# Shorter lists searched from below, and bias-table transfers moved, in a two-block transformer kernel

## The reference, cut to what matters

```python
score = jnp.einsum('bqhk,bqh->bqk', jax.nn.relu(s), wib * idx_scale)
visible = key_chunk[None, :] <= qcb[:, None]
score = jnp.where(visible[None], score, NEG_INF)
_, sel = lax.top_k(score, k_top)                 # k_top = 256
valid = key_chunk[sel] <= qcb[None, :, None]
kg = gather(k, sel)
...
logits = jnp.where(valid[:, :, None, :], logits, NEG_INF)
```

```python
bias = rpb[:, (dr + NA_KH_MAX - 1)[None, :, None], (dc + kw - 1)[:, None, :]]
s = s + bias.astype(jnp.float32)[None]
```

## Time and profile before

| what | value |
|---|---|
| median of 3 runs | 3490.18 us (3487.72 to 3490.66) |
| the profiled execution's own time | 3484.2 us |
| its span | 3482.4 us |
| PE busy in the span | 3266.4 us (94%) |
| DVE busy | 1759.2 us (51%) |
| ACT busy | 1218.6 us (35%) |
| POOL busy | 1180.2 us (34%) |
| mean granted PE clock | 0.972 of full speed |

### The profile page before, as it was taken

One profiled execution on the slowest core, in us unless ns is written; L12 is line 12 of the kernel. 1 busy time (PEld: TensorE's weight loads), 2 busy tenths in 40 slices (PEclk: granted clock), 3 DMA queues, 4 the chain that ended last, 5 costly groups with the idle time before them and its releaser, 6 DMA issues. The chain is left out here.

```text
span 3482.4 us, 43824 instructions
## 1 busy us (share of the span) xinstructions
PE 3266.4 (94%) x17544; PEld 2854.7 (82%) x17544; DVE 1759.2 (51%) x2950; ACT 1218.6 (35%) x1847; POOL 1180.2 (34%) x844
## 2 busy tenths in 40 slices
PE   7899989998998999999998999989899899999997
PEld 6789989988887899999875788777787688888885
DVE  5579999553356799985435044433334321000014
ACT  5552211452265421225414154444423422222222
POOL 4316432115332373311343342311452433333232
PEclk9999999999999999999998999999999899999998
DMA  5111233104310112220141411111332111111111
GB/s 157 27 30 43 60 90 96 53 1 157 108 61 25 37 46 77 86 79 16 65 143 33 169 41 46 37 55 34 104 131 84 43 48 49 49 49 45 47 49 55
DMA packets 292159, 228.52 MB, mean 66 GB/s; under 512 B 37351, under 2 KB 266390, under 8 KB 291574
## 3 DMA queue, kind: packets, MB, share of 16 engines
q1 hardware_dynamic: 264278, 122.38, 13.0%
q0 software_dynamic: 21920, 82.13, 6.3%
q10 hardware_dynamic: 5760, 21.22, 1.5%
HBM read 175.31 MB, written 52.16 MB: 65 GB/s over the span
## 5 line engine op out<-in xcount | busy, mean ns | idle before, releaser
L670 PE MATMUL big<-H,wsp 128*128 128x348 f32 (+3 forms) x9600 | 1905.9, 358 | 70.7 <-POOL H L1786 25.1
L670 PEld LDWEIGHTS big<-H,wsp 128*128 128x128 f32 (+1 forms) x9600 | 1666.0, 191 | 277.1 <-issue 41.4
L1786 POOL TENSOR_TENSOR wsp<-raw,wsp 128x1024 fp32r<-128x1024 f32 (+2 forms) x246 | 542.8, 2207 | 1524.1 <-ACT wsp L1234 1513.4
L670 PE MATMUL big<-SP,wsp 128*128 128x512 f32 x1920 | 452.1, 396 | 0.0
L670 PEld LDWEIGHTS big<-SP,wsp 128*128 128x128 f32 x1920 | 360.3, 188 | 89.8 <-issue 0.7
L1234 ACT ACTIVATE wsp<-raw 128x1024 fp32r<-128x1024 f32 (+2 forms) x246 | 238.1, 968 | 516.3 <-PE big L670 369.2
L2473 DVE MAX8 top<-SC 128x8 f32<-128x272 f32 (+6 forms) x448 | 369.4, 825 | 0.0
L2479 DVE MATCH_REPLACE8 SC<-top,SC 128x272 f32<-128x272 f32 (+6 forms) x448 | 366.0, 817 | 0.0
L2633 DVE TENSOR_TENSOR X<-X,big 128x1024 f32<-128x1024 f32 (+1 forms) x26 | 29.6, 1139 | 478.1 <-PE big L670 478.1
L819 PE MATMUL small<-V,PT_a 128*128 128x64 f32 x1152 | 146.5, 272 | 0.1
L1282 ACT ACTIVATE rows_a<-rows_a,head_min 128x1040 f32<-128x1040 f32 (+8 forms) x130 | 101.6, 782 | 123.9 <-DVE head_min L2224 123.8
(11 more groups left out here) (316 smaller groups left out, 3590.4 us busy)
## 6 DMA issues: line engine op xcount, KB each, us to landing
raw<-in_w_in SPq DMA_DIRECT2D x108, 512.0 KB, 3.8
raw<-in_w_ff SPq DMA_DIRECT2D x64, 512.0 KB, 4.0
raw<-in_w_out SPq DMA_DIRECT2D x24, 512.0 KB, 5.3
gate_b_scratch<-tm POOLq DMA_DIRECT2D x16, 522.0 KB, 3.9
gate_a_scratch<-tm ACTq DMA_DIRECT2D x16, 522.0 KB, 2.8
tm<-gate_a_scratch POOLq DMA_DIRECT2D x16, 522.0 KB, 3.9
tm<-gate_b_scratch POOLq DMA_DIRECT2D x16, 522.0 KB, 4.7
tm<-xT_scratch POOLq DMA_DIRECT2D x16, 522.0 KB, 5.0
```

The costliest lines, as they stand in the source:

```text
L670: mm = pe.matmul(dst(o, width), w[wp][:, k, 0:cols], rhs(xp, k)[:, t0:t0 + width], start=(k == 0 and i == 0), stop=(k == rows - 1 and i == 2))
L1786: pool.tensor_tensor(dst, src, hi.bitcast(F32), ALU.subtract).then_inc(*S.inc(name, *key))
```

## The change

For blocks whose list is shorter than 512 (j = 1 and 2), the search runs on a copy. The copy is the negated scores in reversed order, in a free area that now has the name `low_scores`; it is searched for the keys to be left out, of which there are visible(j) - 256: 16 and 144, that is 2 and 18 rounds of 8. The mask is then read from the copy, reversed again, with the opposite comparison. Blocks 3 to 7 keep their 32 rounds. Reversing makes equal scores fall as before.

All three stages of the bias tables now stand behind one load, (ya, 1) of layer 0, whole: 3 pad transfers, a wait, 24 skewed ones, a wait, 24 strips. The load after them in SP's program is (ya, 2).

```diff
-        sb("z_rest", [P, (2 * KC * SEQ - KC * TP - 2 * TP - 9 * HD - SCORE_COLS)])
+        low_scores = sb("z_rest", [P, (2 * KC * SEQ - KC * TP - 2 * TP - 9 * HD - SCORE_COLS)])
...
-            band_steps = {nload[("mb", 0, 0)]: (lambda: rpb_pad())}
-            for i in range(6):
-                band_steps[nload[("mb", 0, 1)] + i] = lambda i=i: skewed_bands(tables[4 * i:4 * i + 4])
-                band_steps[nload[("mb", 0, 5)] + i] = lambda i=i: strip_bands(tables[4 * i:4 * i + 4])
+
+            band_steps = {nload[("ya", 0, 1)]: lambda: (rpb_pad(), skewed_bands(tables), strip_bands(tables))}
...
+                scores = {j: SC[:, SCORE_AT[j]:SCORE_AT[j] + visible(j)] for j in range(1, NQ)}
+                lowest = {j: visible(j) < 2 * TOPK for j in range(1, NQ)}
+                low_at = {j: sum(visible(i) for i in range(1, j) if lowest[i]) for j in range(1, NQ)}
+                searched = {j: low_scores[:, low_at[j]:low_at[j] + visible(j)] if lowest[j] else scores[j] for j in range(1, NQ)}
+                count = {j: (visible(j) - TOPK if lowest[j] else TOPK) // 8 for j in range(1, NQ)}
+                turned_keys = lambda ap, j: ap[:, visible(j) - 1::-1]
...
-                rounds = [(r, j) for r in range(TOPK // 8) for j in range(1, NQ)]
+                for j in range(1, NQ):
+                    if lowest[j]:
+                        wait(("mask_step", l, "hidden", j))
+                        dve.tensor_scalar(searched[j], turned_keys(scores[j], j), -1.0, None, ALU.mult)\
+                            .then_inc(*S.inc("mask_step", l, "turned", j))
+                rounds = [(r, j) for r in range(TOPK // 8) for j in range(1, NQ) if r < count[j]]
...
-                        dve.match_replace(sc, top8[:, j, :], sc, TAKEN).then_inc(*S.inc("taken", l, r, j))
+                        dve.match_replace(searched[j], top8[:, j, :], searched[j], TAKEN).then_inc(*S.inc("taken", l, r, j))
                 for j in range(1, NQ):
-                    sc = SC[:, SCORE_AT[j]:SCORE_AT[j] + visible(j)]
-                    wait(("taken", l, TOPK // 8 - 1, j))
-                    dve.tensor_scalar(sc, sc, TAKEN / 2, NEG, ALU.is_gt, ALU.mult).then_inc(*S.inc("mask_step", l, "made", j))
+                    wait(("taken", l, count[j] - 1, j))
+                    found = turned_keys(searched[j], j) if lowest[j] else searched[j]
+                    dve.tensor_scalar(scores[j], found, TAKEN / 2, NEG, ALU.is_lt if lowest[j] else ALU.is_gt, ALU.mult)\
+                        .then_inc(*S.inc("mask_step", l, "made", j))
```

More of the change, by code:

```diff
@@ L2471, in _ @@
                         r, j = rounds[x]
-                        wait(("taken", l, r - 1, j) if r else ("mask_step", l, "hidden", j))
-                        dve.max(top8[:, j, :], SC[:, SCORE_AT[j]:SCORE_AT[j] + visible(j)])\
-                            .then_inc(*S.inc("eight", l, r, j))
+                        wait(("taken", l, r - 1, j) if r else ("mask_step", l, "turned" if lowest[j] else "hidden", j))
+                        dve.max(top8[:, j, :], searched[j]).then_inc(*S.inc("eight", l, r, j))
                     if x >= 1:
                         r, j = rounds[x - 1]
-                        sc = SC[:, SCORE_AT[j]:SCORE_AT[j] + visible(j)]
                         wait(("eight", l, r, j))
-                        dve.match_replace(sc, top8[:, j, :], sc, TAKEN).then_inc(*S.inc("taken", l, r, j))
+                        dve.match_replace(searched[j], top8[:, j, :], searched[j], TAKEN).then_inc(*S.inc("taken", l, r, j))
                 for j in range(1, NQ):
-                    sc = SC[:, SCORE_AT[j]:SCORE_AT[j] + visible(j)]
-                    wait(("taken", l, TOPK // 8 - 1, j))
-                    dve.tensor_scalar(sc, sc, TAKEN / 2, NEG, ALU.is_gt, ALU.mult).then_inc(*S.inc("mask_step", l, "made", j))
+                    wait(("taken", l, count[j] - 1, j))
+                    found = turned_keys(searched[j], j) if lowest[j] else searched[j]
+                    dve.tensor_scalar(scores[j], found, TAKEN / 2, NEG, ALU.is_lt if lowest[j] else ALU.is_gt, ALU.mult)\
+                        .then_inc(*S.inc("mask_step", l, "made", j))
                 for j in range(1, NQ):
```

## The result

Over four runs of each the changed kernel takes 3470.77 us in the median (3463.19 to 3478.82), the kernel before 3490.42 (3487.72 to 3491.24). The ratio is 0.994, with a 95% interval of 0.9928 to 0.9952: 0.6% faster, where 3470.9 us and 0.55% were forecast. The changed kernel run again in a later batch gives 3465.75 against 3487.06, ratio 0.9941 (0.9927 to 0.9955).

The account below looks back on a forecast made before the run. PE, busy 94% of the span, was taken as the bound; 12.73 us (tables, layer 0) plus 6.51 (search, layer 1) made 19.24 off, forecasting 3470.9 us, own range 3467 to 3475, wider range 3466 to 3478.

Parts of the forecast that it names:

- The two costs and their coupling: Table transfers cost layer 0 12.73 us and hide its search; late search costs layer 1 6.51; both 19.2.
- the search's lateness in layer 1: Layer 1, unit 0's to unit 3's logits: PE waits for DVE's search, then runs on a slow clock; 6.51 us.
- Why the tables cost PE time: Layer 0's mb jobs: SP issues 24 skewed tables between weight loads, so PE waits for split weights; 12.73 us.
- The sum of the search: DVE, each layer: 37.1 us of search pairs dropped, 1.5 us of copies and reversed masks added; 35.6 us net.
- The chain on SP: Layer 0's attention: pads, skewed tables and strips take 97 us, ending at 702, before (ya, 2) is needed; no cost.
- the bound of 138: Layer 0's attention: table transfers on SP with the dearest issue each time, 138 us, ending at 743; margin 40 us.
- The slower rival: Layer 0: table transfers outlast the attention, (ya, 2) comes late; beyond 178 us PE pays; 205 us gives 3497.2; chance 0.03.
- The gate loads: POOL's four loads in layer 0's attention, 27.3 us slack; rival: delayed in series, giving back 10.7 us, 3481.6; chance 0.05.
- The rival that something comes back inside the attention: Layer 0's attention: traffic beside PE, ACT and DVE handovers gives back a third of the 12.7 us; 3475; chance 0.08.
- The level: Whole kernel: median run time forecast at 3470.9 us, 0.55% less, with its own range 3467 to 3475.

Follow-up runs that it names:

- Search alone: Changed kernel with the bias-table transfers put back among the mb jobs as in the kernel before; 3482.12 against 3487.06 us, ratio 0.9985.
- tables alone: Kernel before with only the table transfers moved behind load (ya, 1) of layer 0, search as before; 3480.92 against 3487.06 us, ratio 0.9983.
- The longer chains: Changed kernel with the skewed-table transfers made twice, 3467.7 us, and three times, 3531.22 us, against 3489.31 for the kernel before.

## Why the prediction was right

**The two costs and their coupling.** Held in all parts. Off the mb jobs 12.73 us were predicted and measured; off the search's lateness in layer 1 6.51 and 6.50. Search alone: 6.5 predicted, 5.2 measured; tables alone: 6.2 and 5.9; both: 19.2 and, from the ratio of 0.994, 20.9 (the medians differ by 19.65). Each made alone, the parts add up to 11.1 us, and together they bring some 20; the remainder, 6.5 predicted and 9 measured, with some 3 us of uncertainty on each part and 4 on the two together, is what the tables' 12.7 us had been hiding of layer 0's search. The timelines show it without the noise: the tables alone lose 5.05 us to it in layer 0, where I had taken layer 1's 6.5; the two stretches differ in that execution (20.54 against 1549.55 - 1527.69 = 21.86), with the same wait of about 3.3 us in each, and the 1.3 us come behind it, where PE's passes are slow for longer in layer 1.

**Why the tables cost PE time.** The prediction had the weights late because SP issues the tables between them; SP's rows in the kernel before bear that out, and show that it is the issuing and not the landing:

```profile
434.72 3.73 SPq L616 DMA_DIRECT2D raw<-in_w_in  x1
438.49 9.56 SPq L592 DMA_DIRECT2D band_scratch<-rpb_scratch  x4
448.11 2.81 SPq L616 DMA_DIRECT2D raw<-in_w_branch_b  x1
```

Four loads, two pairs of an mb and a yb job, take SP from 408.19 to 460.60, 26.2 us a pair, while PE, unhindered, needs 17.2 us for one (yb 0 at 403.05, yb 1 at 420.23). The load issued from 448.11 is split by ACT at 453.91, 3.0 us behind its issue. A load's own issue takes 2.8 to 3.9 us there and 0.37 in the changed kernel; what holds it is not shown.

**The sum of the search.** 35.6 us net were predicted. The masks' last step ends the search; before, then after:

```profile
619.82 0.56 DVE L2486 MEMSET SC<- 64x64 f32 x7
```

```profile
590.62 0.41 DVE L2498 MEMSET SC<- 64x64 f32 x5
```

Counted from yb 0 that is 216.77 us and 181.66, so 35.1 less. There are 180 MAX8 a layer, as said. The pairs were right (block 2's 14 pairs, less its copy, make the idle time 14.2 us longer, from 14.60 to 28.78; 14.3 less a copy was predicted). The copies were mis-sized: 0.5 us each, measured 2.06 for the two from start to start (274.49 to 276.55). Reading in reverse is not the reason: the second copy, reversed as well, takes 0.36 us for 400 columns. The masks read in reverse cost nothing more either: all seven take 3.06 us (587.56 to 590.62) where they took 3.19 (616.63 to 619.82), and the 0.25 us put on each of two was not needed.

**The chain on SP.** 97 us predicted, 98.9 measured (the bound of 138 adds up to 137.3, which changes nothing); from the next load's issue to ACT's split 88 us predicted (702 to 790.4), 85 measured. The longer chains show the margin's end: 170.6 us cost nothing, 246.9 us (608.56 to 855.41) made PE wait 62.5. Counted back one for one, the price begins at some 184 us of chain, where I had put 178. The slower rival is thus a real mechanism, a little farther away than it was put: the load landed in some 3 us where 7 were allowed, and PE's need comes 3.6 us behind ACT's. A long landing of the 32 B runs did not show: landing stays within 5.6 us behind the last issue (615.15 + 73.14 to 693.88).

**The gate loads.** Landed within 7.9 us beside the tables (8.2 in the version with the tables alone), 7.0 without; DVE reads at 676.6 what was issued by 642.3, so over 26 us of slack were left. The rival that something comes back inside the attention has nothing for it: with and without the transfers the stretch agrees to 0.2 us wherever it takes its short time.

**The level.** That 3470.9 meets 3470.8 so closely is luck: the changed kernel spreads over 15.6 us in its first four runs. What I took as its own uncertainty, 3467 to 3475, was too narrow for a single run; the median of the first four lies in it, and that of the five of the later batch, 3465.75, does not. There the kernel before was 3.4 us faster as well, and the ratio is the same.

## What to carry to other kernels

When a kernel runs the same program twice and only one pass has an extra, lay the two timelines side by side from one shared instruction to the next: the extra's cost is the difference. See in other executions how far the stretch varies by itself: yb 0 to unit 0's logits took 210.3 us wherever no tables were in it, but 223.03 and 224.62 in the two executions with them. Before a stall is removed, ask what it was hiding; here 5 of the 12.7 us that the transfers gave back would have gone to the search, and the search alone gave little, because one layer did not need it. Once the later of two arrivals is early, further savings on it (here block 2's 14 us) are worth nothing until the other one moves.

## What the runs showed of the hardware

**The start of the kernel varies by some 6 us.** In the ten profiled executions, whose PE instructions are the same up to there, yb 0 starts at 402.9 to 409.0 us. The first passes of PE differ: in the changed kernel's first profile and in its second,

```profile
24.55 3.43 PE L898 MATMUL small<-SC,allmean 16*128 16x16 f32 x14 [5.24 <-DVE SC L2367]
33.25 4.52 PE L668 MATMUL big<-H,wsp 128*128 128x348 f32 x18 [5.27 <-POOL H L1784]
```

```profile
22.43 2.50 PE L898 MATMUL small<-SC,allmean 16*128 16x16 f32 x14 [2.92 <-DVE SC L2367]
30.20 4.73 PE L668 MATMUL big<-H,wsp 128*128 128x348 f32 x18 [5.27 <-POOL H L1784]
```

They are 3 us apart at the first projection, and 2.1 of these already at the row ahead of it, which waits for one DVE instruction with two inputs in SBUF. What differs is which of two engines started first. The changed kernel's first profile, then its second:

```profile
21.11 2.35 POOL L1784 TENSOR_TENSOR wsp<-raw,wsp 128x1024 fp32r<-128x1024 f32 x1 [16.27 <-ACT wsp L1232]
21.14 3.26 DVE L2367 SCALAR_TENSOR_TENSOR SC<-ident,token_rstd 128x896 f32<-128x896 f32 x1
```

```profile
21.19 1.09 DVE L2367 SCALAR_TENSOR_TENSOR SC<-ident,token_rstd 128x896 f32<-128x896 f32 x1
21.47 3.02 POOL L1784 TENSOR_TENSOR wsp<-raw,wsp 128x1024 fp32r<-128x1024 f32 x1 [16.66 <-ACT wsp L1232]
```

In three of the ten executions POOL is first, by 0.03 to 0.10 us; DVE's instruction then takes 3.19 to 3.26 us and POOL's 2.34 or 2.35. In the other seven DVE is first, by 0.01 to 0.39 us; DVE's takes 1.09 and POOL's 2.91 to 3.29. The three have their yb 0 at 406.9 to 409.0, the seven at 402.9 to 405.8. The rest of the spread builds up later, all of it ahead of 300 us, and was not followed up.

**The attention's end has two times.** The 1.5 to 2 us between the short and the long attentions lie almost wholly in their last ten us. The 5 us that end 5.5 us ahead of ya 0, in layer 0 before and then after (the fields are busy times by engine, the granted clock, the DMA share and GB/s):

```profile
785.00:790.00 5.00, 3.81 (x11) 2.09 (x10) 1.18 (x3) 0.24 (x2) 0.49 (x1) 0.52 0.02 3
```

```profile
776.50:781.50 5.00, 3.00 (x17) 1.83 (x16) 0.99 (x3) 1.48 (x6) 1.46 (x2) 1.00 0.01 3
```

In the long one the granted clock is down at 0.52 there, the lower level of 1.2 GHz, and in the short one still at 1.00. In the 5 us ahead of these, at a granted clock of 1.00 in both, PE was busy for 3.76 us in the long one and for 4.22 in the short. One pass (`small<-meta_v,meta_pt`) takes 2.02 us in the first and 1.08 in the second; in all twenty attentions it takes 1.94 or 2.02 in the long ones and 1.08 in the short. Why the clock falls some microseconds earlier in one execution than in another is not shown. A stretch of the second block, from its first `big<-tm,rot` pass to its first `big<-SP,wsp`, likewise takes 331.9 to 333.4 us in seven executions and 336.0 to 336.2 in three. So spans of single profiles differ by several us for reasons that have nothing to do with an edit, and are to be compared stretch by stretch.

**DVE's and POOL's instructions hold each other up.** Besides the one at the start, a short one at the head of each search is long. The first reversed copy takes 1.87 or 1.93 us, the one behind it 0.29 to 0.36. POOL's timeline at the time, changed kernel first, then the version with the other order of copies:

```profile
273.49 2.71 POOL L1784 TENSOR_TENSOR wsp<-raw,wsp 128x1024 fp32r<-128x1024 f32 x1 [23.42 <-ACT wsp L1232]
```

```profile
272.62 2.71 POOL L1784 TENSOR_TENSOR wsp<-raw,wsp 128x1024 fp32r<-128x1024 f32 x1 [23.64 <-ACT wsp L1232]
```

POOL's instruction ends at 276.20 and 275.33, the copy that started at 274.49 and 273.62 ends 0.16 and 0.2 us after it. The Trainium skill ("SBUF — State Buffer", SBUF: two separate sides) says that VectorE and GpSimd share a pair of ports, and that a VectorE instruction in a two-port mode, or with two SBUF inputs against a GpSimd instruction that reads SBUF, and the GpSimd instruction exclude each other: whichever starts first holds the pair for its whole instruction, and the other waits. The start of the kernel agrees in both directions: 1.09 us against 3.19 to 3.26 for DVE's instruction, 2.34 against 2.91 to 3.29 for POOL's, by who came first. By that rule the copy, if it runs in a two-port mode, waits; the traces agree in both orders of the copies, in both layers. That the copy runs in such a mode no run shows by itself, and the copies with POOL idle were not tried, so for them the cause is argued. The hold costs 1.5 us of DVE time here, in its idle time.
